# Five matmuls a tile instead of six, first conditioning chunks in pairs, and the queries' norm applied in the exponential, in a four-layer diffusion trunk on one core

## What is computed

```python
for i in range(DEPTH):                       # kinds: attn, pool, fnet, attn
    sh1, sc1, g1, sh2, sc2, g2 = ada_mods(cond, ada_w[i], ada_b[i])   # silu(cond) @ w + b
    h = modulate(rmsnorm(x, norm_mix[i]), sh1, sc1)                    # h * (1 + scale) + shift
    if kind == 0:
        q, k, v = split(h @ attn_w_qkv)                 # 16 query heads, 4 key heads of 64
        q, k = rmsnorm(q, q_norm), rmsnorm(k, k_norm)   # per head
        o = attention(rope(q), rope(k), v, sink)        # scale 64 ** -0.5, window 128, sink logit
        mix = o @ attn_w_o
    ...
    x = x + g1 * mix
    h = modulate(rmsnorm(x, norm_ffn[i]), sh2, sc2)
    u = depthwise_conv3(h @ ffn_w_in) + b               # 5632 channels
    x = x + g2 * ((silu(gate) * val) @ ffn_w_out)
```

## Time and profile before

| | |
|---|---|
| median of 3 runs | 2840.65 us (2839.8 to 2843.64) |
| the profiled execution | 2844.42 us |
| its span | 2842.6 us |
| mean granted TensorE clock | 0.978 |
| TensorE busy | 2742.6 us, 96% of the span |
| weight loads on TensorE | 2595.9 us |
| VectorE busy | 1573.7 us, 55% |
| ScalarE busy | 1154.9 us, 41% |
| POOL busy | 123.2 us, 4% |

### The profile page before, as it was taken

One profiled execution on the slowest core, in us unless ns is written; L12 is line 12 of the kernel. 1 busy time (PEld: TensorE's weight loads), 2 busy tenths in 40 slices (PEclk: granted clock), 3 DMA queues, 4 the chain that ended last, 5 costly groups with the idle time before them and its releaser, 6 DMA issues.

```text
span 2842.6 us, 49930 instructions
## 1 busy us (share of the span) xinstructions
PE 2742.6 (96%) x19584; PEld 2595.9 (91%) x19584; DVE 1573.7 (55%) x2665; ACT 1154.9 (41%) x1924; POOL 123.2 (4%) x151
## 2 busy tenths in 40 slices
PE   5989999999998999999899999999998999999999
PEld 4966999999998999999879999999998789999999
DVE  2678366536635664465342665366367946653662
ACT  3357354324425551343232543244244845532440
POOL 1000100000012000000201000000100010000000
PEclk8989899999999999999999999999998999999999
DMA  6123233233321433333201333233221012222222
GB/s 258 60 94 135 83 119 141 107 109 137 143 84 49 145 124 113 119 143 123 84 0 60 126 141 106 110 133 143 73 75 49 2 38 67 74 77 71 71 81 78
DMA packets 62471, 280.48 MB, mean 99 GB/s; under 512 B 7392, under 2 KB 9568, under 8 KB 49632
## 3 DMA queue, kind: packets, MB, share of 16 engines
q1 hardware_dynamic: 62304, 278.07, 27.3%
HBM read 274.88 MB, written 3.16 MB: 98 GB/s over the span
## 4 chain that ended last, share of the span: by engine, by line
PE 91%; DVE 5%; ACT 2%; issue 1%; SPq 1%; DMA 1%; POOL 0%; POOLq 0%; DVEq 0%; ACTq 0%
PE ps L513 77%; PE ps L621 3%; PE ps L716 2%; PE ps L812 2%; PE ps L702 2%; PE ps L687 1%; PE ps L571 1%; DVE prob L1329 1%; PE ps L749 1%; PE ps L579 1%; DMA first_w<-in_ada_w 1%; DVE prob L1345 1%; PE ps L549 1%; DVE h_lo L1186 1%; PE ps L795 0%
## 5 line engine op out<-in xcount | busy, mean ns | idle before, releaser
L513 PE MATMUL ps<-h_hi,w_hi 128*128 128x322 f32 x3552 | 832.5, 316 | 5.6 <-DVE h_lo L1385 1.8
L513 PE MATMUL ps<-h_lo,w_hi 128*128 128x322 f32 x3552 | 823.0, 313 | 0.0
L513 PE MATMUL ps<-h_hi,w_lo 128*128 128x322 f32 x3552 | 817.7, 311 | 0.0
L873 ACT ACTIVATE w_hi<-w_raw 128x1024 fp32r<-128x1024 f32 (+1 forms) x288 | 325.6, 1130 | 1110.4 <-PE ps L513 975.9
L513 PEld LDWEIGHTS ps<-h_hi,w_hi 128*128 128x128 f32 x3552 | 599.0, 190 | 32.1 <-issue 24.7
L513 PEld LDWEIGHTS ps<-h_lo,w_hi 128*128 128x128 f32 x3552 | 605.2, 190 | 0.0
L513 PEld LDWEIGHTS ps<-h_hi,w_lo 128*128 128x128 f32 x3552 | 604.9, 190 | 0.0
L1131 DVE TENSOR_TENSOR w_lo<-w_raw,w_hi 128x1024 fp32r<-128x1024 f32 (+1 forms) x288 | 379.0, 1316 | 118.0 <-ACT w_hi L873 116.2
L1249 DVE SCALAR_TENSOR_TENSOR x<-ps,mods,x 128x321 f32<-128x321 f32 (+5 forms) x264 | 99.8, 434 | 508.1 <-PE ps L513 508.1
L513 PE MATMUL ps<-f_hi,w_hi 128*128 128x322 f32 x1408 | 325.7, 313 | 0.0
L513 PE MATMUL ps<-f_lo,w_hi 128*128 128x322 f32 x1408 | 324.0, 311 | 0.0
(11 more groups left out here) (120 smaller groups left out, 2176.8 us busy)
## 6 DMA issues: line engine op xcount, KB each, us to landing
ada_w<-in_ada_w SPq DMA_DIRECT2D x90, 1024.0 KB, 5.3
w_raw<-in_w_in SPq DMA_DIRECT2D x176, 512.0 KB, 3.2
w_raw<-in_w_out SPq DMA_DIRECT2D x64, 704.0 KB, 4.0
w_raw<-in_w_qkv SPq DMA_DIRECT2D x24, 512.0 KB, 3.2
w_raw<-in_w_o SPq DMA_DIRECT2D x16, 512.0 KB, 3.2
first_w<-in_ada_w SPq DMA_DIRECT2D x6, 1024.0 KB, 15.3
w_raw<-in_w_fnet SPq DMA_DIRECT2D x8, 512.0 KB, 3.3
x<-in_x SPq DMA_DIRECT2D x1, 2576.0 KB, 10.2
```

The lines of the kernel that those rows point to most:

```text
L513: mm = pe.matmul(ps[:, 2 * par + hf, 0:NH], w[par][:, kk, :], b[:, hf * NH:(hf + 1) * NH], start=(kk == 0 and n == 0), stop=(kk == k - 1 a ...
L873: act.activation(w_hi[par][:, 0:k, :], w_raw[par][:, 0:k, :], ACT.Copy).then_inc(hi_made, 1)
```

## The change

- **Tiles.** `h_hi`, `h_lo` and `f_hi`, `f_lo` are interleaved in one tensor (`h[:, kk, 0 or 1, :]`). The shift columns move into the pads, so 642 columns are left. The first 386 (MAIN) go to one bank in three matmuls of 386. Of the last 256 (TAIL), w_hi times high and low part are one matmul of 512 columns that reads the two parts in two runs and writes them side by side; w_lo times the high part (256 columns) is added to the first half.
- **Taking the product.** ScalarE copies the second half out of PSUM (`tail_copy`, ahead of `split_hi`), VectorE adds the first half (`add_tails`). `rescale` is three instructions instead of one, `update` four instead of three, with a wait between.
- **Start.** Chunks j and j+4 come as pair j, which gives shift and scale of channel tiles 2j and 2j+1; after each pair the tiles before it of units 0 and 1 are multiplied. `conv` is loaded last, the first weights ahead of the last six chunks.
- **Queries.** Only the two key tiles go through `invert`, `turn_heads` and `rotate`. The rotary tables are multiplied by the query gain once a layer (`query_tables`); a query tile gets its rotary turn alone (`query`), and its inverse norm is the scale of the exponential (`q_scale`) and of the maximum (`neg_scale`). POOL multiplies the sink by the root. The value tiles are turned after units 5 and 8, and the last query tile is turned after the first `masked`.

```diff
-                    b_hi, b_lo = rhs(kk)
-                    for n, (w, b) in enumerate(((w_hi, b_hi), (w_hi, b_lo), (w_lo, b_hi))):
-                        for hf in range(2):
-                            mm = pe.matmul(ps[:, 2 * par + hf, 0:NH], w[par][:, kk, :],
-                                           b[:, hf * NH:(hf + 1) * NH],
-                                           start=(kk == 0 and n == 0), stop=(kk == k - 1 and n == 2))
+                    mm = products(par, kk, rhs(kk), kk == 0, kk == k - 1)
...
+            def products(par, kk, b, first, last):
+                main, wide = ps[:, 2 * par, 0:MAIN], ps[:, 2 * par + 1, :]
+                wh, wl = w_hi[par][:, kk, :], w_lo[par][:, kk, :]
+                pe.matmul(main, wh, b[:, 0, 0:MAIN], start=first, stop=False)
+                pe.matmul(main, wh, b[:, 1, 0:MAIN], start=False, stop=False)
+                pe.matmul(wide, wh, b[:, :, MAIN:NT], start=first, stop=last, skip_group_check=True)
+                pe.matmul(main, wl, b[:, 0, 0:MAIN], start=False, stop=last)
+                return pe.matmul(wide[:, 0:TAIL], wl, b[:, 0, MAIN:NT], start=False, stop=last,
+                                 skip_group_check=True)
...
+            def tail_copy(u, par):
+                act.wait_ge(unit_done, u + 1)
+                act.activation(tail_low[par][:], ps[:, 2 * par + 1, TAIL:2 * TAIL], ACT.Copy).then_inc(tail_copied, 1)
...
+            def add_tails(u, par):
+                dve.wait_ge(tail_copied, u + 1)
+                dve.tensor_tensor(tail[par][:], ps[:, 2 * par + 1, 0:TAIL], tail_low[par][:],
+                                  ALU.add).then_inc(tail_added, 1)
+                dve.wait_ge(tail_added, u + 1)
...
             def rescale(u, par):
                 dve.wait_ge(unit_done, u + 1)
-                dve.tensor_tensor(halves(scaled[par][:]), product(par), halves(rstd[:]),
+                dve.tensor_tensor(scaled[par][:, 0:MAIN], ps[:, 2 * par, 0:MAIN], rstd[:, 0:MAIN], ALU.mult)
+                add_tails(u, par)
+                dve.tensor_tensor(scaled[par][:, MAIN:NT], tail[par][:], rstd[:, MAIN:NT],
                                   ALU.mult).then_inc(taken[par], 1)
...
-            for c in range(FIRST_CHUNKS):
-                ada_multiply(0, c, c % 2, chunk_turn(c))
-            ada_turn(0)
+            for j in range(FIRST_PAIRS):
+                for b in range(2):
+                    ada_multiply(j, b, b, 0)
+                ada_turn(j)
+                if j:
+                    first_unit_tiles(j - 1)
             pe.wait_ge(const_in, 16 * len(CONSTS))
+            sum_squares(0, False)
+            for s in range(2):
+                for kk in (KT - 2, KT - 1):
+                    first_tile(s, kk)
+                    if (s, kk) == (1, KT - 2):
+                        turn_back(0)
...
-                        if n >= 3:
+                        if n in (3, 4):
                             turn_heads(layer, n - 3)
-                    sum_heads(layer, 9)
...
+                    def query(tile):
+                        n = Q0 + tile
+                        dve.wait_ge(q_root, KT * a + tile + 1)
+                        dve.reciprocal(q_scale[:, tile, :, :], q_rms[:, tile, :, :]).then_inc(q_inv, 1)
+                        dve.wait_ge(qkv_out, 12 * a + n + 1)
+                        prompt = qkv[:, n, CTX0:CTX0 + CTX]
+                        dve.tensor_scalar(prompt, prompt, head_gain[:, a, 0:1], None, ALU.mult)
+                        dve.wait_ge(q_inv, KT * a + tile + 1)
+                        dve.tensor_scalar(neg_scale[:, tile, :, :], q_scale[:, tile, :, :], -1.0, None,
+                                          ALU.mult).then_inc(q_scaled, 1)
+                        turn_pairs(qkv[:, n, LAT0:LAT0 + LAT])
...
-                                           bias=st[:, 1:2], scale=HD ** -0.5,
+                                           bias=st[:, 1:2], scale=q_scale[:, tile, nb, hd:hd + 1],
```

313 lines of the change are left out of this document (183 added, 130 removed).

## The result

The changed kernel took 2815.06 us (median of 4 runs, 2814.9 to 2817.33). In the same rounds the kernel before took 2841.53 us (4 runs, 2839.8 to 2843.64). The ratio is 0.991, with a 95% interval from 0.9893 to 0.9924. The profiled execution took 2814.92 us and its span is 2813.1 us, so the span fell by 29.5 us. The forecast for it was 58.8.

A forecast was written before the change was run, and what follows sets the result against it. TensorE's unit matmuls were taken to bound the kernel (77% of the span); -44.6 (tiles) - 15.7 (queries) - 6.5 (start) + 7 (taking the product) + 1 (last layer) = -58.8 us, giving a 2781.8 us median, range 2766 to 2812.

The forecast's parts named there:

- The tile: All 2480 unit tiles: five matmuls instead of six gain 18 ns each, 44.6 us (43 to 48).
- so it hardly grows with the columns: Step in the tile's price: the time above a matmul's columns is nearly constant, 14.9 ns at 322 columns, 13.8 at 512.
- The bounds of 17.4 and 19.5: Gain per tile in ns: lower from 6 columns plus one fixed cost, upper from a straight line through both paces.
- The two-run operand: Wide matmul reading two runs: price between nothing and 14.9 ns a tile (37 us); taken as nothing.
- rival 2: Weight load not covered by the 256-column matmul, which keeps 149 ns instead of 121: slower, 2851 us median; chance 0.05.
- Rival 1: A tile gains little, through a two-run cost or an overhead not tied to matmul count: 2818 to 2820 us; chance 0.13.
- The last layer: Up-projection: longer rescales use up VectorE's 1.35 us slack per two units; 1 us lost.
- Rival 3: VectorE sets the pace in the last layer's up-projection: 2792 us; chance 0.10, inside the range.
- Queries: Attention layers: fewer turns on TensorE and earlier steps after unit 11 gain 7.85 us per layer, 15.7 in two.
- Start: Kernel start: paired chunks let early tiles run beside transfers, unit 2 starting at 56.6 instead of 63.31; 6.5 us gained.
- Taking the product elsewhere: Norms and kernel end: longer rescale, update and copy not covered, plus 1.5 us for the clock; 7 us lost (3 to 12).
- The clock: After norms, longer idle time may let the clock fall: 1.5 us added to the loss.

The follow-up runs named there:

- The stretches by themselves: Rows of 96 equal matmuls run alone behind the changed kernel's own work: 117.5 ns for 256 columns, 148.2 for 322, 231.7 for 512, 232.9 in two runs.
- the layouts: Changed kernel with the SiLU later and input rows 656 columns apart, starting 2, 14 or 0 columns after a 64-byte multiple: 2791.89, 2797.42, 2820.26 us.
- 24 layouts: Stretches of 32 five-matmul tiles behind the kernel's own work, rows 642 to 688 columns apart, starts 0, 2 or 14: start 0 took 887.7 to 896.1 ns.

## Why the prediction was wrong, point by point

The sum for the span was -58.8 us and the trace has -29.5.

- **What bounds it** was right: TensorE in the units. That this stayed so in the last layer was not.
- **The tile: -44.6 forecast, -29.2 measured**, 15.4 short. The last layer's 12.9 ns times 2480 would be 32.0; over the whole kernel the 2186 tiles that are followed directly by the next in both traces take 882.2 ns instead of 894.0, which is 11.8 each. The step that failed is "so it hardly grows with the columns". It took 14.9 ns from one size at one place and 13.8 from another size at another, and made a constant of their agreement. The stretches by themselves show 10.8 ns on top of 256 columns, 14.0 on 322 and 18.4 on 512 (19.6 in two runs), and the place of the rows moves a tile of five by 20 more. The bounds of 17.4 and 19.5 had one mechanism in both, the count of matmuls; the spread in this kernel, by the layouts, is from 5 ns (890) to 24 ns (870.7) of gain. The two-run operand, for which I took nothing, costs 1.2 ns in the stretches, its start not being the same; the cover of the weight load was whole, with 117 to 122 ns for 256 columns, so rival 2 fell. Rival 1 came true in part: the wide matmul is at 232 ns, between the 227 of the forecast and the 240 that would have shown the rival.
- **The last layer: +1 forecast, 9.1 measured.** Rival 3 came true in its price, with 14.54 us a pair as against TensorE's 14.11 (0.43 where the prediction had 0.5), but not in its cause, since VectorE waited and wasn't short of time. The step counted VectorE's two `rescale`s against its slack of 1.35 us, and left out ScalarE's queue: the copy is an instruction there, and behind the SiLU. What stands ahead of the copy on ScalarE was never asked; the copy was booked only as what "delays `split_hi`".
- **Queries: -15.7 forecast.** With six matmuls everywhere, the two attention layers came out 6.4 and 7.0 us shorter, 13.4 together. After unit 11 the first and the second `masked` start 5.6 and 10.4 us after `rescale` (forecast 6.3 and 11.2), so the order was read rightly. That a pointer for a constant costs nothing there failed: 3.8 us.
- **Start: -6.5 forecast, -5.3 measured** at unit 2 (57.98 instead of 63.31), and 1.8 to 5.5 at the first key unit's sum over all versions with this start.
- **Taking the product elsewhere: +7 forecast, +3.7 measured** (12.9 less 9.2). VectorE takes 1.36 us for the three instructions of a `rescale`, as forecast (after unit 11 of layer 0, from 141.39 to 142.75). The idle time before the sums of squares was 2.95 us as foreseen:

```profile
1552.71 2.29 PE L571 MATMUL ps<-ones,sq_sum 128*128 128x1 f32 x10 [2.95 <-POOL sq_sum L481]
```

- **The clock** adds little. These ten matmuls take 1.28 us at full clock and 2.28 at a granted clock of 0.50, the 1.2 GHz level. They were slow at the second norms of layers 0 and 3 before, and at the norm ahead of layer 1 and the second norms of layers 2 and 3 after. From a norm's sum to the first conditioning chunk behind it takes 10.5 to 10.8 us where the granted clock stays at 1.00 (1574.94 to 1585.75 in the kernel before), 12.2 to 12.3 with 3.4 us at 0.50, and 13.3 to 13.9 with 5.7 to 6.8 us at 0.50. From layer 0's second norm to the norm ahead of layer 3 the clock stood at 0.50 for 34.1 us before and for 37.5 after. That makes at most 1.7 us, half of the difference.
- **The sum** of what is measured is -29.2 + 9.1 - 13.4 - 5.5 + 3.7 = -35.3 us, and 5.8 us are left. At most 1.7 are the clock's, and some 4 I can't assign. A part lies where a tile is followed by something else. Without the second half of the product the stretch between those two norms is 15.7 us shorter than before: its 1472 plain tiles gave 17.0 us, 11.5 ns each, but the 176 that have a conditioning chunk, a norm's sum, a mixer or an end of a unit behind them took 1.8 us more, where 12.9 ns each would have taken off 2.3.
- **The range** missed by 3 us. It let rival 1 in only by half, and had no case in which the tile and the last layer both fall short. The figure that the prediction gave beside its sum by the 2.5 ns of the Trainium skill ("TensorE: Matmul & The Clock Gate", the section on the 56 ns gap), 2814, is near the result by chance: it had 12 us for the tiles, which gave 29, and 14 us for all other terms together, which nearly cancelled.

What the experiments leave open is why the place of the operand counts. They show that it does and by how much: the start relative to 512 bytes and the distance both enter. They also leave open whether the Fourier layer's 227.1 ns come from the place, since only six starts within 64 bytes were tried for 512 columns.

## What to carry to other kernels

The pace of a stream of matmuls is worth a measurement at the sizes and at the addresses that the changed kernel will have: with 2480 tiles, 1 ns is 2.5 us, and a shift of the rows by two columns moved this kernel by 28 us, about as much as the whole change brought. An instruction added on a helper engine is to be placed in its queue, not only in its sum of busy time; the copy of 0.37 us cost 9 us because it stood behind a SiLU that waited for VectorE, and nothing once the two were exchanged. A scalar read from memory in place of a constant is an operand with a price, 89 ns on ScalarE and 59 on VectorE here.

## What the runs showed of the hardware that was not expected

- A float32r matmul of 512 columns takes 227.1 ns in the Fourier layer and 231.7 ns from `h`; with the starts 0 to 12 columns after a multiple of 64 bytes 232.4 to 239.9.
- Five equal matmuls of 386, 386, 512, 386 and 256 columns take from 870 to 896 ns a tile by where their operands lie, six of 322 columns from 893.7 to 897.2.
- Rows that start on a multiple of 64 bytes were the slowest of three starts at each of eight distances.
- Tiles of five whose rows have one distance and start at the same place relative to 512 bytes took the same time within 0.25 ns, whatever their weights and data (60 pairs in 24 layouts); those that agree only relative to 64 bytes differed by up to 26 ns.
